# Attention masks copied into PSUM ahead of the scores, scores two pairs and maxima one pair ahead

## What is computed

```
def fox_attention(q, k, v, f_logit):
    c = jnp.cumsum(jax.nn.log_sigmoid(f_logit), axis=1)
    for blk in range(T // Q_BLOCK):                 # two query blocks of 128
        logits = einsum('bhqd,bhkd->bhqk', qh[s0:end], kh[:end])
        logits = logits + c[s0:end] - c[:end]       # forget bias per key
        p = softmax(where(mask, logits, -inf)); out = p @ vh[:end]
def mla_mixer(...):
    s = q_nope . k_nope + q_pe . k_pe               # 64 + 32 rows of contraction
    p = softmax(where(causal, s * scale, -1e30)); out = p @ v
```

## Time and profile before

| | us |
|---|---|
| median of 3 runs | 2331.27 (2328.78 to 2338.29) |
| the profiled execution's own time | 2329.94 |
| its span | 2328.1 |
| fox attention, first score product to the projection behind it | 506.58 to 550.34 |
| mla attention, the same | 887.62 to 925.09 |
| mean granted clock of TensorE | 0.989 of full speed |

### The profile page before, as it was taken

One profiled execution on the slowest core, in us unless ns is written; L12 is line 12 of the kernel. 1 busy time (PEld: TensorE's weight loads), 2 busy tenths in 40 slices (PEclk: granted clock), 3 DMA queues, 4 the chain that ended last, 5 costly groups with the idle time before them and its releaser, 6 DMA issues.

```text
span 2328.1 us, 64689 instructions
## 1 busy us (share of the span) xinstructions
PE 2251.5 (97%) x29054; PEld 2008.1 (86%) x29054; DVE 617.2 (27%) x1531; ACT 452.2 (19%) x1031; POOL 42.2 (2%) x31
## 2 busy tenths in 40 slices
PE   7999999999999999999987999999999999999998
PEld 6878888757888876888875889999999999999998
DVE  3424323323432345211469120101010111111111
ACT  3422111213211134101033121111111111111111
POOL 0000000000000000000024000000000000000000
PEclk9999999999999999999998999999999999999999
DMA  7133333241334322333422159999999999999996
GB/s 315 73 131 120 135 155 145 80 174 64 119 143 162 113 88 113 148 131 155 163 110 91 55 210 387 358 379 363 362 374 362 371 354 383 344 387 344 397 353 260
DMA packets 103108, 522.04 MB, mean 224 GB/s; under 512 B 8369, under 2 KB 8498, under 8 KB 95410
## 3 DMA queue, kind: packets, MB, share of 16 engines
q1 hardware_dynamic: 102962, 519.82, 58.2%
HBM read 518.74 MB, written 1.05 MB: 223 GB/s over the span
## 4 chain that ended last, share of the span: by engine, by line
PE 91%; DVE 6%; ACT 2%; issue 1%; DMA 0%; SPq 0%; DVEq 0%; ACTq 0%
PE ps L1521 25%; PE ps L989 18%; PE ps L1535 13%; PE ps L968 10%; PE ps L1000 10%; PE ps L1046 3%; PE ps L1212 1%; PE ps L1508 1%; DVE scr L2062 1%; PE ps L1014 1%; PE ps L1479 1%; PE ps L1155 1%; DVE rstd L1645 1%; PE ps L1198 1%; PE ps L1243 1%
## 5 line engine op out<-in xcount | busy, mean ns | idle before, releaser
L1521 PE MATMUL ps<-scr,slot 128*64 128x96 f32 x14336 | 638.0, 246 | 3.6 <-issue 2.6
L1521 PEld LDWEIGHTS ps<-scr,slot 128*64 128x64 f32 x14336 | 612.3, 137 | 5.0 <-issue 4.8
L989 PE MATMUL ps<-hT,slot 128*128 128x256 f32 x2016 | 445.4, 379 | 0.0
L989 PEld LDWEIGHTS ps<-hT,slot 128*128 128x128 f32 x2016 | 383.0, 190 | 52.1
L1535 PE MATMUL ps<-scr,slot 128*64 128x96 f32 x7168 | 343.0, 247 | 0.3 <-issue 0.3
L1535 PEld LDWEIGHTS ps<-scr,slot 128*64 128x64 f32 x7168 | 314.9, 137 | 24.7 <-issue 24.6
L1000 PE MATMUL ps<-scr,slot 128*128 128x256 f32 x1056 | 238.9, 379 | 2.3 <-DVE scr L1887 2.3
L1000 PEld LDWEIGHTS ps<-scr,slot 128*128 128x128 f32 x1056 | 200.3, 190 | 31.0 <-DVE scr L1887 3.9
L2191 DVE TENSOR_TENSOR scr<-scr,ps 128x96 f32<-128x96 f32 x224 | 56.5, 252 | 612.6 <-PE ps L1521 612.6
L829 ACT ACTIVATE scr<-ps 128x96 f32<-128x96 f32 x224 | 56.3, 251 | 825.5 <-PE ps L1521 825.5
L968 PE MATMUL ps<-hT,slot 128*128 128x256 f32 x736 | 170.9, 388 | 2.3 <-ACT hT L509 1.4
(11 more groups left out here) (352 smaller groups left out, 1467.1 us busy)
## 6 DMA issues: line engine op xcount, KB each, us to landing
slot<-in_w_moe SPq DMA_DIRECT2D x224, 1024.0 KB, 7.1
slot<-in_w_moe SPq DMA_DIRECT2D x224, 512.0 KB, 7.0
slot<-in_w_ffn SPq DMA_DIRECT2D x33, 3072.0 KB, 10.2
slot<-in_w_even_in SPq DMA_DIRECT2D x4, 3072.0 KB, 23.0
slot<-in_w_odd_qk SPq DMA_DIRECT2D x2, 3072.0 KB, 10.0
slot<-in_w_s_glu SPq DMA_DIRECT2D x2, 3072.0 KB, 10.0
slot<-in_w_odd_v SPq DMA_DIRECT2D x2, 2048.0 KB, 8.6
slot<-in_w_even_out SPq DMA_DIRECT2D x1, 3072.0 KB, 10.1
```

Source lines behind the costliest of these rows:

```text
L989: m = pe.matmul(pair(f, k), w[:, o:o + P], hT[:, c], start=c == 0, stop=c == KD - 1, skip_group_check=True)
L1521: m = pe.matmul(pair(f, k)[s:s + STRIP, 0:CAP], w[:, o:o + STRIP], xg[e % 2][:, c], start=c == 0, stop=c == KD - 1, skip_group_check=True)
```

## The change

The mask is no longer multiplied in by TensorE behind each pair's scores, but lies in the bank before the scores are made, and every score product accumulates onto it.

- GpSimd builds `mask3` (128x384: mask, zeros, mask) once in SBUF, after the first mixer. It takes a place that `mag_` had; `mag_` moves.
- For pairs 0 and 1 TensorE writes `mask3` into the two banks (identity times 384 columns, one product a head). For pairs 2 to 7 ScalarE copies it into the bank: `biased(p)` waits for the exponents of pair p and makes two copies of 128x384 into the banks of pair p + 2. It stands first in ScalarE's list of pair p, behind `turned(p - 1)` and `mixed(p - 2)`.
- TensorE makes `scores(p + 2)` in front of pair p's work, no longer `scores(p + 1)`, and waits there for the two copies in place of the exponents. VectorE takes the maxima of pair p + 1 ahead of `turned(p - 1)` and `normalize(p)`.
- The semaphore of the scores is raised by the last product onto each head's bank (L1243, or the last L1277).

```
--- before
+++ after
+                def biased(p):
+                    act.wait_ge(at["exp"], n0 + 2 * p + 2)
+                    for h in (2 * p, 2 * p + 1):
+                        act.activation(ps[:, 4 + h % 4, 0:3 * P], mask3, ACT.Copy
+                                       ).then_inc(at["biased"], 1)
                 for p in range(HEADS // 2):
+                    if p + 2 < HEADS // 2:
+                        biased(p)
                     if p + 1 < HEADS // 2:
                         exponents(2 * p + 2)
                         exponents(2 * p + 3)
                     turned(p)
                     if p:
                         mixed(p - 1)
...
                 def scores(p):
+                    heads = (2 * p, 2 * p + 1)
                     if p >= 2:
-                        pe.wait_ge(at["exp"], n0 + 2 * p - 2)
-                    heads = (2 * p, 2 * p + 1)
+                        pe.wait_ge(at["biased"], b0 + 2 * p - 2)
+                    else:
+                        for h in heads:
+                            pe.matmul(ps[:, 4 + h % 4, 0:3 * P], ident, mask3, start=True, stop=False,
+                                      skip_group_check=True)
                     products(heads)
-                    for h in heads:
-                        for c in (0, 2 * P):
-                            m = pe.matmul(ps[:, 4 + h % 4, c:c + P], ident, mask, start=False,
-                                          stop=True, skip_group_check=True)
-                        m.then_inc(at["scores"], 1)
...
                 scores(0)
+                scores(1)
                 for p in range(HEADS // 2):
-                    if p + 1 < HEADS // 2:
-                        scores(p + 1)
+                    if p + 2 < HEADS // 2:
+                        scores(p + 2)
...
+                maximum(0)
+                maximum(1)
                 for p in range(HEADS // 2):
-                    maximum(2 * p)
-                    maximum(2 * p + 1)
+                    if p + 1 < HEADS // 2:
+                        maximum(2 * p + 2)
+                        maximum(2 * p + 3)
...
+            pool.wait_ge(mix_ready, KD)
+            for b in (0, 2):
+                pool.tensor_copy(mask3[:, b * P:(b + 1) * P], mask).then_inc(at["maskmade"], 1)
+            pool.memset(mask3[:, P:2 * P], 0.0).then_inc(at["maskmade"], 1)
```

More of the change, by code:

```diff
@@ L290, in build_program @@
         at = {n: sem("at_" + n) for n in (
-            "flog", "fscaled", "rcol", "rcoltaken", "fbias", "logsig", "c", "vtile", "vtaken", "scores", "max", "exp", "prob",
+            "flog", "maskmade", "biased", "fscaled", "rcol", "rcoltaken", "fbias", "logsig", "c", "vtile", "vtaken", "scores", "max", "exp", "prob",
             "pturned", "eventaken", "oddtaken", "out", "posrow", "poscol", "reduced", "trig", "turned", "roped")}
@@ L329, in build_program @@
         qpe_raw = part(12, 4).rearrange("p (a n) -> p a n", a=4)
-        kpe, cos, sin, ang, turns, red, mag_ = (part(16 + i) for i in range(7))
+        kpe, cos, sin, ang, turns, red, mag_ = (part(i) for i in (16, 17, 18, 19, 20, 21, 11))
+        mask3 = part(22, 2)[:, 0:3 * P]
         posf = scr[0:1, 24 * T:25 * T]
@@ L630, in mixed @@
                     act.activation(mixT[:, p], ps[:, p % 2, 0:T], ACT.Copy).then_inc(mix_ready, 1)
+                act.wait_ge(at["maskmade"], 3)
                 exponents(0)
@@ L1145, in attention @@
                 p0 = n0 // 2
+                b0 = 0 if kind == "fox" else HEADS - 4
                 def scores(p):
+                    heads = (2 * p, 2 * p + 1)
                     if p >= 2:
-                        pe.wait_ge(at["exp"], n0 + 2 * p - 2)
-                    heads = (2 * p, 2 * p + 1)
-                    products(heads)
-                    for h in heads:
-                        for c in (0, 2 * P):
-                            m = pe.matmul(ps[:, 4 + h % 4, c:c + P], ident, mask, start=False,
-                                          stop=True, skip_group_check=True)
-                        m.then_inc(at["scores"], 1)
+                        pe.wait_ge(at["biased"], b0 + 2 * p - 2)
[3 more added lines that the diff above has]
+                                      skip_group_check=True)
+                    products(heads)
                 def turn(h):
@@ L1182, in attention @@
                 pe.wait_ge(at["vtaken"], 4 if kind == "fox" else 8)
+                pe.wait_ge(at["maskmade"], 3)
                 scores(0)
+                scores(1)
                 for p in range(HEADS // 2):
-                    if p + 1 < HEADS // 2:
-                        scores(p + 1)
+                    if p + 2 < HEADS // 2:
+                        scores(p + 2)
                     if p:
@@ L1199, in head_products @@
                                   proj[r:r + HD, h // 2, qb * P:(qb + 1) * P],
-                                  proj[r:r + HD, 8 + h // 2, 0:(qb + 1) * P], start=qb == 0,
+                                  proj[r:r + HD, 8 + h // 2, 0:(qb + 1) * P], start=False,
                                   stop=False, skip_group_check=True)
@@ L1243, in products @@
                         pe.matmul(ps[:, 4 + h % 4, 0:3 * P], one.to_broadcast([HEADS, P]), negc,
-                                  start=False, stop=False, skip_group_check=True)
+                                  start=False, stop=True, skip_group_check=True
+                                  ).then_inc(at["scores"], 1)
                 attention("fox", products)
@@ L1276, in products @@
                             r = ROPE * (h % 4)
-                            pe.matmul(ps[:, 4 + h % 4, qb * P:(2 * qb + 1) * P],
+                            m = pe.matmul(ps[:, 4 + h % 4, qb * P:(2 * qb + 1) * P],
                                       proj[r:r + ROPE, 16 + h // 4, qb * P:(qb + 1) * P],
-                                      kpe[r:r + ROPE, 0:(qb + 1) * P], start=False, stop=False,
+                                      kpe[r:r + ROPE, 0:(qb + 1) * P], start=False, stop=qb == 1,
                                       skip_group_check=True)
+                            if qb:
+                                m.then_inc(at["scores"], 1)
                 attention("mla", products)
```

## The result

The changed kernel takes 2365.73 us, the median of 4 runs (2365.03 to 2370.21), against 2332.51 of the kernel before (2328.78 to 2338.29, 4 runs): a ratio of 1.0145, 95% interval 1.0130 to 1.0161. It is slower by about 1.4%, and its time lies above the upper end of the predicted range (2363).

The account below looks back on a forecast made before the run. The prediction took TensorE, busy 97% of the span and alone on the attentions' chain, as the bound. 2329.9 + 1.6 at full clock + 14 for fox's clock gave 2345.5, median 2347 us, range 2330 to 2363.

Parts of the forecast that it names:

- What goes and what it would be worth: Both attentions: six pairs each lose TensorE's mask product, 13.1 us; less 1.6 for entry masks, a gain of 11.5 us.
- The ring: Each later pair: TensorE waits for ScalarE's mask copies, queued behind copies awaiting TensorE's transposes; 5.34 us fox, 4.71 mla.
- The mask copy: ScalarE's copy of 384 mask columns into PSUM, taken as 488 ns from a row with as many columns.
- The Trainium skill's faster way into PSUM: ScalarE's mask copies: PSUM is a faster destination than SBUF, which would put the sum up to 2.4 us lower.
- At full clock +1.6 us: Both attentions at 2.4 GHz: fox 43.6 against 43.8, mla 39.3 against 37.5, together 1.6 us slower.
- The last scores of mla at 29.5: End of mla's pairs at full clock: last scores begin 29.5 us after its start, against 28.6 before.
- So I take it that the clock falls in fox and holds in mla: TensorE's clock drops to 1.2 GHz in fox only, after idle time and narrow products; chance 0.50, range 2337 to 2356.
- the stretch at 886.85: Earlier mla trace: idle 0.77 us, then narrow products, clock held; taken as nearest to mla's new pairs.
- falls in both: Rival: the clock falls in mla as well as fox, about 16 us more, 2363; chance 0.13.
- The price of the fall in fox: Fox at 1.2 GHz: 20 us if lasting from behind the third pair, 7 if in the last pairs only; 14 taken.
- The Trainium skill against the trace: TensorE's clock in the attentions: by the skill it holds, leaving +1.6 us; the trace fell after a 0.87 us gap.

Follow-up runs that it names:

- the ring open: Changed kernel with ScalarE's mask copies placed ahead of its copy of transposes; 2337.01 us, ratio 1.0028 to the kernel before.
- with 128 rows: Changed kernel with fox's forget bias product over 128 rows in place of 16; 2350.08 us, ratio 1.0064 to the kernel before.
- the kernel with the wait moved: Changed kernel with ScalarE's wait for the mask ahead of the copies of the values; 2347.22 us, ratio 1.0060 to the kernel before.
- with the ring opened and 16 rows: Changed kernel with mask copies ahead of the copy of transposes and ScalarE's mask wait moved, forget bias still 16 rows; 2327.71 us, ratio 0.9988.
- filled: Changed kernel with unused 128-row products added behind each pair's transposes and ahead of the third scores; 2340.26 us, ratio 1.0028.
- ring alone: Changed kernel with ScalarE's mask wait moved and fox's forget bias over 128 rows, mask copies left in place; 2338.29 us, ratio 1.0033.
- all three: Changed kernel with mask copies ahead of the copy of transposes, ScalarE's mask wait moved and forget bias over 128 rows; 2325.73 us, ratio 0.9974.

## Why the prediction was wrong, step by step

- **What goes and what it would be worth.** Right. With the ring open, the pairs last 3.95 us in fox, as forecast, and 3.32 in mla until the other engines bind.
- **The ring.** Right: forecast 5.34 and 4.71 us a pair at full clock and 8.2 in fox at 1.2 GHz, measured 5.34 (with 128 rows), 4.71 and 8.47; idle 1.39 forecast, 1.32 measured. Reading ScalarE's list, not its busy share of 19%, gave this.
- **The mask copy.** Right: L629 has a mean of 495 ns, the L637 beside it 491. The Trainium skill's faster way into PSUM ("ScalarE: Activation LUTs", section "Step-by-step: what each stage is for") does not show: the copy into PSUM is no shorter than the copy out of it.
- **At full clock +1.6 us.** Near, in part by luck. Fox is 43.5 (forecast 43.6) and mla 39.8 (39.3) without the late table load, so +2.0 in the two attentions; with it and 128 rows fox is 44.3. The last scores of mla at 29.5 don't follow from the terms written down: the working shown for fox gives 28.8 there. The 0.7 that is too much stands near a wait that I hadn't named, 0.58 in front of mla's third scores, and measured (in the kernel with the wait moved) it is 29.7.
- **"So I take it that the clock falls in fox and holds in mla": the first half right, the second wrong.** This is the first of two steps that failed. Mla fell too, 47.8 us against the 39.3 of the step, 8.5 more. I leaned on the stretch at 886.85 in the earlier trace rows, which had a single idle time of 0.77 us and was followed by the 128-row L1155; the new mla has a wait of 1.87 in front of its third scores, 1.32 in every pair at full clock, and no L1155. The rival "falls in both", with a chance of 0.13, is what happened; but that its 2363 is near the measured 2365.7 is luck. It put 16 us on mla and 14 on fox, and measured were 8.5 and 22.5.
- **The price of the fall in fox.** Mis-sized, the second step that failed. I took 14 us, between a fall in the last pairs (7) and one behind the third pair that lasts (20). It fell during the third pair's scores (at 518.2) and came back only in the projection: fox 64.6 instead of 43.6 and 1.5 in the projection, 22.5 us. The upper end was the measured one, and no row spoke for averaging it with a late fall. In both profiles with the ring and 16 rows fox stayed down for 58.0 us; mla came back inside its ring after 10.2 us, and after 27.3 and 34.1 in two other kernels. Why the one stays down and the other doesn't is open. Each of the two misses is worth 8.5 us; either alone would have left the time at about 2356, inside the range.
- **Not seen: the table load.** The prediction put nothing on ScalarE's new wait for the mask. It moved the 1.28 us load behind the first maximum, which made the third scores wait 0.60 us longer in fox and 1.3 longer in mla. Whether it also cost mla its clock is not shown (see the experiment).
- **The Trainium skill against the trace.** The Trainium skill ("TensorE: Matmul & The Clock Gate", section "Why this matters for your kernels") ties a fall in mid-kernel to idle gaps longer than any here, as the prediction said. The trace disagrees more plainly than the prediction could: in the changed kernel's fox the clock fell with no gap above 0.60 us since its first mask product, and with the ring opened and 16 rows it fell with none.

What stays open: why the clock falls and holds at different places from run to run, and how much of the spread of most kernels here, 10 us or more, that is; one execution of each has a profile. Three of the four profiles whose fox held (filled, ring alone, all three) came to fox some 6 us later than the others, at 514.2 to 514.8, after longer stretches at 1.2 GHz near 111 to 129 us; only the 128 rows at 508.50 are like for like with the changed kernel. Open is also whether GpSimd's three small operations, which now lie at about 143 to 150 us, have a part in the 3.4 to 6.8 us at 1.2 GHz that six of the eight profiles with `mask3` show near there and neither of the two without it. These six reach fox at 508.5 or later, the other four at 506.6 to 507.3; so the 1.9 us by which the changed kernel's fox starts late may belong to it. That was not tried.

## What to carry to other kernels

Before moving work from a busy engine to an idle one, walk the loop through the new instruction: what stands in front of it in its engine's list, and what does that wait for? If the answer is the busy engine itself, shortly before it will need the result, the idle engine's whole list is on the chain. Put the work behind the last thing that it truly depends on, not where the pair begins. And ask what a saved full-array product did for TensorE's clock: here the loop was left with narrow products and idle time, and lost more to the clock than the saving was worth.

## What the runs showed of the hardware

- With the same instructions and columns and no less idle time, 16 rows of contraction let the granted clock fall to 1.2 GHz (fox 64.6 us) and 128 rows, 112 of them zero weights, held 2.4 GHz (44.3 us), at no cost in time: 1.48 and 1.49 us a pair at 2.4 GHz.
- 1.4 us of useless 128-row products in place of each of the ring's waits made the kernel 25 us faster than the changed one.
- The longest idle time of the changed kernel's fox between its first mask product and its fall was 0.60 us, in front of the third scores; with the ring opened and the wait moved, fox still fell, with no idle time in those 10 us; with the 16-row product widened, idle times of 1.32 us in the same attention were followed by no fall.
